# The gate product of a hybrid decoder layer: seven half-size products in place of eight

## The reference, cut to what matters

```
ff = square(relu(hn @ w_up));  h = h + rms_norm(ff @ w_down, mlp_post_g)
gate = sigmoid(h @ w_ple_gate + b_ple_gate)          # (512 x 1024) @ (1024 x 1024)
ple  = (p @ w_ple) * gate
out  = h + rms_norm(ple, ple_post_g)
```

## Time and profile before

| | |
|---|---|
| median of 3 runs | 583.5 us (583.44 to 583.79) |
| span of the profiled execution, first to last instruction | 581.5 us |
| busy in that span | PE 573.5, DVE 495.2, ACT 356.4, POOL 98.6 us |
| granted clock of TensorE, mean | 0.996 |
| time of the profiled execution as a whole | not listed apart from its span; it is read with the runs, whose median lies 2.0 us above the span |

### The profile page before, as it was taken

One profiled execution on the slowest core, in us unless ns is written; L12 is line 12 of the kernel. 1 busy time (PEld: TensorE's weight loads), 2 busy tenths in 40 slices (PEclk: granted clock), 3 DMA queues, 4 the chain that ended last, 5 costly groups with the idle time before them and its releaser, 6 DMA issues.

```text
span 581.5 us, 8919 instructions
## 1 busy us (share of the span) xinstructions
PE 573.5 (99%) x3400; PEld 500.8 (86%) x3400; DVE 495.2 (85%) x639; ACT 356.4 (61%) x569; POOL 98.6 (17%) x152
## 2 busy tenths in 40 slices
PE   8999999999999999999999999999999999999995
PEld 7888888888888888989999999999989999988885
DVE  5899986688766998999989999999999899799664
ACT  6896675775646746667656665575655756654422
POOL 0331536000103463001010011010100100011011
PEclk9999999999999999999999999999999999999998
DMA  8982008223003559469485492774753936584011
GB/s 269 345 320 85 0 2 324 76 72 123 25 1 109 202 189 319 87 183 229 96 249 114 119 276 41 215 185 74 264 132 75 285 75 155 207 294 178 0 73 73
DMA packets 26250, 89.26 MB, mean 154 GB/s; under 512 B 3040, under 2 KB 4448, under 8 KB 25696
## 3 DMA queue, kind: packets, MB, share of 16 engines
q1 hardware_dynamic: 20448, 66.59, 32.6%
q0 software_dynamic: 4032, 14.68, 14.3%
q10 hardware_dynamic: 1728, 7.42, 3.4%
HBM read 82.40 MB, written 6.29 MB: 153 GB/s over the span
## 4 chain that ended last, share of the span: by engine, by line
PE 98%; DMA 1%; DVE 0%; ACT 0%; SPq 0%; issue 0%; POOL 0%; DVEq 0%; ACTq 0%
PE psum L2340 31%; PE psum L2344 30%; PE psum L2345 30%; PE psum L2395 2%; PE psum L2578 2%; PE psum L2558 2%; DMA first_raw_a<-weights_dram 1%; PE psum L2409 1%; PE psum L2432 0%; DVE h L1323 0%; ACT w_hi L1393 0%; POOL stat L2192 0%; PE psum L2463 0%; PE psum L2457 0%; PE psum L2437 0%
## 5 line engine op out<-in xcount | busy, mean ns | idle before, releaser
L2340 PE MATMUL psum<-t_hi,a_hi 128*128 128x512 f32 x216 | 84.8, 393 | 0.0
L2344 PE MATMUL psum<-t_lo,a_hi 128*128 128x512 f32 x216 | 84.6, 392 | 0.0
L2345 PE MATMUL psum<-t_hi,a_lo 128*128 128x512 f32 x216 | 84.0, 389 | 0.0
L2340 PE MATMUL psum<-w_hi,actT_hi 128*128 128x512 f32 (+1 forms) x190 | 73.6, 387 | 0.0
L2345 PE MATMUL psum<-w_hi,actT_lo 128*128 128x512 f32 (+1 forms) x190 | 72.4, 381 | 0.0
L2344 PE MATMUL psum<-w_lo,actT_hi 128*128 128x512 f32 (+1 forms) x190 | 72.3, 380 | 0.0
L2345 PE MATMUL psum<-sum_hi,up_lo 128*128 128x256 f32 x224 | 63.4, 283 | 0.0
L2344 PE MATMUL psum<-sum_lo,up_hi 128*128 128x256 f32 x224 | 63.4, 283 | 0.0
L2340 PE MATMUL psum<-sum_hi,up_hi 128*128 128x256 f32 x224 | 63.2, 282 | 0.0
L2345 PE MATMUL psum<-actT_hi,up_lo 128*128 128x256 f32 (+1 forms) x200 | 60.0, 300 | 0.0
L2344 PE MATMUL psum<-actT_lo,up_hi 128*128 128x256 f32 (+1 forms) x200 | 60.0, 300 | 0.0
(11 more groups left out here) (264 smaller groups left out, 1415.8 us busy)
## 6 DMA issues: line engine op xcount, KB each, us to landing
raw<-weights_dram SPq DMA_DIRECT2D x34, 512.0 KB, 4.5
raw_o<-weights_dram SPq DMA_DIRECT2D x23, 512.0 KB, 4.3
raw_x<-weights_dram POOLq DMA_DIRECT2D x21, 512.0 KB, 5.6
raw_second<-weights_dram SPq DMA_DIRECT2D x14, 512.0 KB, 4.2
raw_x<-weights_dram SPq DMA_DIRECT2D x9, 512.0 KB, 5.9
qk_raw<-weights_dram SPq DMA_DIRECT2D x8, 512.0 KB, 6.8
gate_raw<-weights_dram SPq DMA_DIRECT2D x8, 512.0 KB, 5.1
raw_o<-weights_dram POOLq DMA_DIRECT2D x7, 512.0 KB, 7.1
```

What stands on the lines that cost most here:

```text
L2340: begin = nc.tensor.matmul(out, a_hi, b_hi, start=first, stop=False, skip_group_check=read_between)
L2344: nc.tensor.matmul(out, a_hi, b_lo, start=False, stop=False, skip_group_check=read_between)
L2345: return nc.tensor.matmul(out, a_lo, b_hi, start=False, stop=last, skip_group_check=read_between)
```

## The change: what it does

The diff, cut to its core:

```diff
+GATE_SPLITS = (GATE_11, GATE_T1, GATE_21, GATE_T2, GATE_T3, GATE_T4, GATE_22)
+GATE_PRODUCTS = ((0, 0), (1, 0), (0, 1), (1, 1), (2, 0), (3, 0), (2, 1), (3, 1), (4, 0), (4, 1), (5, 0), (5, 1),
+                 (6, 0), (6, 1))
+TOKENS_DONE = (2, 3, 0, 1)
...
             def gate_split_lo(block, part):        # DVE, 128x1024
+                dve.wait_ge(block_hi, gate_split_at(block, part))
+                nc.vector.tensor_tensor(gate_half(low, part), gate_source(block, part),
+                                        gate_half(high, part).bitcast(F32), ALU.subtract).then_inc(block_lo, 1)
+            def gate_c22(j):
+                dve.wait_ge(c_copied, gate_copy_at(COPY_E, j))
+                dve.wait_ge(up_filled, gate_at(4, j))
+                part = acc[:, 2 + j, W:2 * W]
+                nc.vector.tensor_tensor(part, part, psum[:, GATE_CHAIN + j, :], ALU.subtract).then_inc(c_summed, 1)
...
             add_mlp(3)                              # DVE's order from here on
-            splits(SLAB_GATE + KD + 4)
-            h2_turn_lo(4)
-            h2_turn_lo(5)
-            splits(SLAB_GATE + KD + 6)
-            h2_turn_lo(6)
-            h2_turn_lo(7)
...
-            for i, (t, c0, width) in enumerate(GATE_TILES):
-                gate_bias(i)
...
-                gate_ple(i)
+            gate_split_lo(GATE_T2, 0), gate_split_lo(GATE_T2, 1)
+            h2_sum(OF_E, 0), h2_sum(OF_S2, 0), h2_sum_split_lo(OF_E, 0), h2_sum(OF_S3, 0), h2_sum_split_lo(OF_S2, 0)
+            gate_c11(0), gate_split_lo(GATE_T3, 0), gate_split_lo(GATE_T3, 1), h2_split_lo(5)
+            h2_sum(OF_E, 1), h2_sum(OF_S2, 1), h2_sum_split_lo(OF_E, 1), h2_sum_split_lo(OF_S2, 1)
+            h2_sum(OF_S3, 1), h2_sum_split_lo(OF_S3, 0), gate_split_lo(GATE_T4, 0), gate_split_lo(GATE_T4, 1)
+            gate_c11(1), h2_sum_split_lo(OF_S3, 1), h2_sum(OF_S4, 0), gate_fold(0), h2_split_lo(7), gate_c22(0)
+            h2_sum(OF_S4, 1), h2_sum_split_lo(OF_S4, 0), gate_split_lo(GATE_22, 0), gate_split_lo(GATE_22, 1)
+            gate_ple(0), gain_ple(0), h2_sum_split_lo(OF_S4, 1), gate_fold(1), gate_c22(1)
+            gate_ple(1), gain_ple(1), gate_ple(2), gain_ple(2), gate_ple(3), gain_ple(3)
+            gate_ple(4), add_ple(2), gate_ple(5), add_ple(3), gate_ple(6), add_ple(0)
+            gate_ple(7), gain_ple(7), gate_ple(8), add_ple(1)
...
+            gate_copy(COPY_C11, 0)                  # ACT's order, the part on sums and results
+            h2_copy_raw(4), h2_copy_raw(5), h2_split_hi(5), h2_sum_split_hi(OF_E, 0), h2_sum_split_hi(OF_S2, 0)
+            gate_copy(COPY_C11, 1), gate_split_hi(GATE_T3, 0), gate_split_hi(GATE_T3, 1)
+            h2_copy_raw(6), h2_copy_raw(7), h2_split_hi(7), h2_sum_split_hi(OF_E, 1), h2_sum_split_hi(OF_S2, 1)
+            gate_copy(COPY_E, 0), gate_copy(COPY_CHAIN, 0), h2_sum_split_hi(OF_S3, 0)
+            gate_split_hi(GATE_T4, 0), gate_split_hi(GATE_T4, 1), h2_sum_split_hi(OF_S3, 1)
+            gate_copy(COPY_E, 1), gate_copy(COPY_CHAIN, 1), sigmoid(0), h2_sum_split_hi(OF_S4, 0)
+            gate_split_hi(GATE_22, 0), gate_split_hi(GATE_22, 1), h2_sum_split_hi(OF_S4, 1)
+            sigmoid(1), square_ple(0), sigmoid(2), square_ple(1), sigmoid(3), square_ple(2), square_ple(3)
+            for i in range(4, len(GATE_TILES)):
                 sigmoid(i)
                 square_ple(i)
...
+            add_gate(GATE_T1, 0), add_gate(GATE_T1, 1)          # POOL
+            nc.gpsimd.tensor_tensor(gate_bias_row[:, W:2 * W], ...)
+            add_gate(GATE_T2, 0), down_rstd(0), add_gate(GATE_T2, 1), down_rstd(1), down_rstd(2)
+            add_gate(GATE_T3, 0), down_rstd(3), add_gate(GATE_T3, 1), add_gate(GATE_T4, 0), add_gate(GATE_T4, 1)
```

More of the change, by code:

```diff
@@ L223, in tail_results @@
             (("down", 5), 1), (("h2T", 0), 2), (("h2T", 1), 3), (("down", 6), 4), (("down", 7), 5),
[L224 to L227, removed]
+            (("h2T", 2), 6), (("h2T", 3), 7), (("h2T", 4), 6), (("h2T", 5), 7), (("h2T", 6), 6), (("h2T", 7), 7)]
     return [name for name, _ in late], dict(late)
@@ L519, in ring @@
                 return (slab // KD % 2) * KD + slab % KD
[L520 to L523, removed]
+            return KD + slab - SLAB_PLE
         def gain_of(slab):
@@ new lines, in h2_sum @@
+            def h2_sum(which, j):
+                a11, a12, a21, a22 = h2_block(0, 0, j), h2_block(0, 1, j), h2_block(1, 0, j), h2_block(1, 1, j)
+                if which == OF_E:
+                    dve.wait_ge(h2_raw, 6 + 2 * j)
+                    first, second, how = a21, a22, ALU.subtract
+                elif which == OF_S2:
+                    dve.wait_ge(x_summed, gate_sum_at(OF_E, j))
+                    first, second, how = gate_e[:, j], a11, ALU.subtract
+                elif which == OF_S3:
+                    first, second, how = a11, a21, ALU.subtract
+                else:
+                    dve.wait_ge(x_summed, gate_sum_at(OF_S2, j))
+                    first, second, how = a12, gate_s2[:, j], ALU.add
+                nc.vector.tensor_tensor(gate_sum_source(which, j), first, second, how).then_inc(x_summed, 1)
@@ L1338, in _ @@
             tail_down(1)
-            splits(SLAB_GATE + 6)
+            gate_split_lo(GATE_T1, 1)
             tail_down(2)
@@ new lines, in _ @@
+            h2_sum(OF_S2, 0)
+            h2_sum_split_lo(OF_E, 0)
+            h2_sum(OF_S3, 0)
+            h2_sum_split_lo(OF_S2, 0)
+            gate_c11(0)
+            gate_split_lo(GATE_T3, 0)
+            gate_split_lo(GATE_T3, 1)
+            h2_split_lo(5)
+            h2_sum(OF_E, 1)
+            h2_sum(OF_S2, 1)
+            h2_sum_split_lo(OF_E, 1)
+            h2_sum_split_lo(OF_S2, 1)
+            h2_sum(OF_S3, 1)
+            h2_sum_split_lo(OF_S3, 0)
+            gate_split_lo(GATE_T4, 0)
@@ new lines, in _ @@
+            gate_split_lo(GATE_T4, 1)
+            gate_c11(1)
+            h2_sum_split_lo(OF_S3, 1)
+            h2_sum(OF_S4, 0)
+            gate_fold(0)
+            h2_split_lo(7)
+            gate_c22(0)
+            h2_sum(OF_S4, 1)
+            h2_sum_split_lo(OF_S4, 0)
+            gate_split_lo(GATE_22, 0)
+            gate_split_lo(GATE_22, 1)
+            gate_ple(0)
+            gain_ple(0)
+            h2_sum_split_lo(OF_S4, 1)
+            gate_fold(1)
+            gate_c22(1)
+            gate_ple(1)
@@ L1381, in _ @@
+            gain_ple(1)
+            gate_ple(2)
+            gain_ple(2)
+            gate_ple(3)
+            gain_ple(3)
+            gate_ple(4)
+            add_ple(2)
+            gate_ple(5)
+            add_ple(3)
+            gate_ple(6)
+            add_ple(0)
+            gate_ple(7)
+            gain_ple(7)
+            gate_ple(8)
+            add_ple(1)
         @block.scalar
@@ L1964, in sigmoid, with gate_copy @@
+            def gate_copy(which, j):
+                product, target, bank = {COPY_C11: (0, acc[:, j, 0:W], GATE_CHAIN),
+                                         COPY_E: (2, acc[:, 2 + j, W:2 * W], GATE_E),
+                                         COPY_CHAIN: (3, acc[:, j, W:2 * W], GATE_CHAIN)}[which]
+                act.wait_ge(up_filled, gate_at(product, j))
+                nc.scalar.activation(target, psum[:, bank + j, :], ACT.Copy).then_inc(c_copied, 1)
             def sigmoid(i):
@@ L1990, in _ @@
             square_down(2)
-            act.wait_ge(filled, filled2["down", 7])
-            act.dma_start(gate_rows[:], rows["gate"]).then_inc(gate_rows_loaded, 16)
-            h2_turn_hi(2)
-            h2_turn_hi(3)
+            for i in (2, 3):
+                h2_copy_raw(i)
+                h2_split_hi(i)
             square_down(3)
-            gate_hi(6)
-            h2_turn_hi(4)
-            h2_turn_hi(5)
-            gate_hi(7)
-            h2_turn_hi(6)
-            h2_turn_hi(7)
-            for i in range(len(GATE_TILES)):
+            gate_split_hi(GATE_T2, 0)
@@ L2004, in _ @@
+            sigmoid(1)
+            square_ple(0)
+            sigmoid(2)
+            square_ple(1)
+            sigmoid(3)
+            square_ple(2)
+            square_ple(3)
+            for i in range(4, len(GATE_TILES)):
                 sigmoid(i)
```

458 lines of the change are left out of this document (332 added, 126 removed).

## The result

The changed kernel took 594.92 us (median of 4 runs, 594.33 to 596.14) beside 583.64 us before (583.44 to 584.03): 1.0196 times as long, 95% interval 1.0181 to 1.0210, or 11.3 us. The forecast was 589.3 us with a range to 594.0: the right sign, and half the size. The profiled execution took 594.33 us with a span of 592.6 us, against the span of 581.5 before.

The account below looks back on a forecast made before the run. DVE's in-order stream was taken as the bound, hiding PE's gain of 5.6 us: profiled span 581.5 + 5.3 (later end) + 0.5 (transfers) = 587.3, and runs lie 2.0 above the span, so 589.3 us; range 585.7 to 594.0.

Parts of the forecast that it names:

- PE saves 5.6 us, and it is hidden: PE after 542.16: 27.5 us of matmuls in place of 33.1, a gain of 5.6 us hidden behind DVE.
- DVE's stream is the bound, by its count: DVE from 535.8: 40 us of work plus root waits, ending later than the last add did before; chance 0.77.
- the walk: Following the PE, DVE and ACT streams in order from 535.8: `gate_ple(0)` at 559.8, the end 5.3 us later.
- The rest from `gate_ple(0)` on, 23 us to the last adds: DVE's epilogue from `gate_ple(0)` at 559.8 to the last adds at about 582.8, with three root waits of 1.16 us.
- What DVE did before 535.72 keeps its size.: DVE ahead of the rewritten stretch: six pairs of slabs split there before and after, so no change in time.
- The bias sum on POOL [...] I take nothing.: Bias sum on POOL: 0.6 to a few us, its bank needed only at 542.16, so priced at 0.
- The transfers, "I take 0.5": The 512 KB adds for T1 and T3, landing 5.6 us after issue in the median: 0.5 us in the sum.
- The price of a late add: T1's first half has 6.3 us from issue to need on ACT; each microsecond beyond shifts all of DVE.
- a late add starves everything: Rival: T1's or T3's adds take 8.2 to 10.6 us, DVE then PE stand still, 591.3 to 596; chance 0.14.
- The drain with the table load: Rival: ACT's table load drains about 1.38 us more, DVE waits 0.8 us, time 590.1; chance 0.01.
- Sums of the prediction: Its totals: 2.3 us of waits before `gate_ple(0)`, DVE's end at 580.0, 2.5 or 7.3 us for slow adds.

Follow-up runs that it names:

- e5: e3 with 24 more matmuls of 512 columns on PE, into a bank nobody reads, ahead of the last product: 589.11 us, 5.5 over before.
- e3: The changed kernel with embedding halves and gain row loaded behind the last gate weights, and the bias sum on DVE instead of POOL: 589.18 us, 6.0 over before.
- e6: e3 without gain_ple for tiles 0 to 3, four DVE operations fewer: 587.81 us, 4.2 over before.
- e1: The changed kernel with embedding halves and gain row (2.5 MB) loaded behind the last gate weights, not right after down 7: 589.89 us, 6.7 over before.
- e2: The changed kernel with the sum of the two bias halves on DVE, not on POOL: 594.67 us, 11.5 over before.
- e10: The changed kernel with only the second embedding half (1 MB) loaded behind the last gate weights: 591.46 us, 8.2 over before.
- e7: The changed kernel with T3's splits moved behind E and S2 of token pair 1 on ACT and DVE, loads unmoved: 589.48 us, 5.8 over before.
- e4: e3 with the epilogues of tokens 2, 3, 0 interleaved and ACT's next sigmoid ahead of each square: 586.98 us, 3.8 over before.
- e9: e4 with C11 formed in PSUM by ACT's copy and PE's adding, and gate_c22(0) one operation later: 588.02 us, 4.8 over before.
- e11: e3 with products (5,0) and (4,1) exchanged on PE, so that the pairs alternate: 589.24 us, 6.0 over before.

## Why the prediction was wrong

- *PE saves 5.6 us, and it is hidden.* Right. e5 gives 24 matmuls back at no cost, and PE ends 11 us before the last adds in e3.
- *DVE's stream is the bound, by its count.* Right. e3 stands 6.0 us over before, where the walk without its transfers gave 5.3; the times at which its operations stand agree within 0.5 us, and that 0.5 is the later start. e6 shows the same from the other side.
- *The rest from `gate_ple(0)` on, 23 us to the last adds.* Right to 0.1 us, and wait by wait: three of 1.16 or 1.17 us for the root, as counted.
- *"What DVE did before 535.72 keeps its size."* Nearly: its operations do, but a wait of 0.46 us for the root of token 3 is new, and the new stream starts 0.6 us later in e3, most of it by this wait.
- *"The bias sum on POOL [...] I take nothing."* Wrong. It was priced by POOL's time and by when its result is needed, not by what it does to DVE beside it: the split beside it took 1.83 us longer. At the start of the new stream some 0.5 us of this was left. In the run times it is not clear of the noise (0.7 between e1 and e3, nothing in e2).
- *The transfers, "I take 0.5".* This is the term that failed, by size: 0.5 us in the sum, 3.42 us of waiting on DVE and 4.6 us of the time when measured. The prediction named the place, T3's second add beside the embedding loads, counted 10.7 us for load and add by the medians against 12.3 to spare, and took 0.5 us. The load was no trouble (3.1 us); the add alone took 10.7 us, and DVE waited 3.42 us. The cause is the 2.5 MB issued ahead of it: without them the add took at most 7.0 us and the kernel 4.6 us less (e1). The medians of the earlier trace rows come from stretches with no such burst. An estimate was in the same rows: 1 MB took 3.4 us longer than 512 KB, so 2.5 MB, five times 512 KB, fill some 17 us. The last of the three loads did take 14.7.
- *The price of a late add.* The prediction let each microsecond beyond the slack shift DVE by one. It did more: the 3.4 us hole also stopped PE for 3.4 us, its clock fell, which took 1.6 us of PE's time, and DVE's wait for product (4,0) became 2.31 us in place of 0.8. In e10, where the hole on PE was 1.16 us and the clock stayed, that wait was 0.80. e7 shows that this hangs on the order of the streams, not on PE's need.
- *A rival, "a late add starves everything", 591.3 to 596,* was what happened for T3, with a chance of 0.14, and the range to 594.0 cut it short. The sign that the prediction named for it, DVE idle for several us before 560 behind ACT's rounding of T3, is in the trace.
- *The drain with the table load.* No. In the changed kernel ACT goes from the last copy over the load to the sigmoid without a wait; its rows stand behind this list. The Trainium skill (ScalarE: Activation LUTs, "What ACT_TABLE_LOAD costs") counts about 1.38 us of drain more, which this trace does not show.
- *Sums of the prediction.* The waits it names ahead of `gate_ple(0)` add up to 2.2 us, not 2.3. DVE's work and root waits from 535.8 on end at 580.2, not 580.0. For adds of 8.2 and 10.6 us its own slacks give 2.9 and 7.7 us, where it has 2.5 and 7.3. None of this changes the outcome.

```profile
558.75 0.60 ACT L2194 ACTIVATE acc<-psum 128x512 f32<-128x512 f32 x1 [2.12 <-PE psum L2652]
559.36 1.28 ACT L2202 ACT_TABLE_LOAD   x1
560.66 0.63 ACT L2202 ACTIVATE acc<-acc 128x512 f32<-128x512 f32 x1
```

In sum, for `gate_ple(0)`, predicted at 559.8 and measured at 565.6: 1.15 from the later start (0.5 POOL's sum, 0.6 the root of token 3), 3.42 from the transfer, 1.5 from product (4,0), less 0.5 of small waits that were shorter than counted. That is 5.6 of the 5.8 us. The rest is in how a wait is counted: from the end of an operation, which lies 0.08 us behind the pace of the walk. No version tried here beats the kernel before: the best, e4, stands 3.8 us over it.

## What to carry to other kernels

Before matrix work is traded for sums and splits, add up the in-order stream of the engine that makes them, from the point where its new work begins to the last operation; where that sum passes the old end, nothing that TensorE saves will show. Price a transfer by the bytes issued ahead of it, and an added byte higher than a loaded one, not by the median of calmer stretches, and put the operation that waits for it behind all those that don't need it. A cost of half a microsecond can't be read from run times that scatter by 2 us, so read it from the start times in several traces (e2, e3).

## What the runs showed of the hardware

- POOL and DVE operations took longer beside each other: 1.83 us more on a DVE split beside a 1.63 us sum on POOL, and the other way round 1.16 in place of 0.27 us for a one-column POOL operation beside DVE's adds.
- An accumulating transfer of 512 KB took 5.3 us at best, and 10.7 to 11.0 us behind 2.5 MB of loads. A MB in such transfers took 1.8 times the DMA engines' time of a MB in plain loads (527 to 552 us of the changed kernel).
- TensorE's granted clock fell, for part of the time to the level of 1.2 GHz, with the end of the hole of 3.43 us: 0.67 in 551 to 552, a mean of 0.83 over the 8 us behind. Holes of 2.24 us before product (5,1) went both ways: behind the ones of e3 and of the changed kernel (2.23) it stayed at 1.00, behind those of e1, e2, e4, e5, e7 and e10, as long and at the same product, it fell to about 0.50 for some two microseconds. What tells them apart was not tested. Behind the holes of 0.94 to 1.66 us in e6, e9, e10 and e11 it stayed at 1.00.

e5, then e3:

```profile
564.00:566.00 2.00, 2.00 (x5) 1.62 (x6) 1.93 (x4) 1.58 (x4) 0.00 (x0) 0.50 0.04 12
```

```profile
564.00:566.00 2.00, 2.00 (x10) 1.62 (x10) 1.93 (x4) 1.68 (x4) 0.00 (x0) 1.00 0.02 4
```
